# Conv taps handed from GpSimd to VectorE and TensorE, with ScalarE writing the diagonals

## The reference

```python
def conformer_conv(u, dw_w, dw_b, norm_g, norm_b):
    a, gate = jnp.split(u, 2, axis=-1)
    z = a * jax.nn.sigmoid(gate)
    z = depthwise_conv(z, dw_w, width 31, centred) + dw_b     # 512 channels
    return silu(layer_norm(z, norm_g, norm_b))

def attn_conv_mixer(x, ...):
    q, k, v, u = split(x @ w_in)
    q, k = rope(rms_norm(q)), rope(rms_norm(k))               # 8 query heads, 2 key heads
    attn = softmax(q k^T / 8) v
    return concat([attn, conformer_conv(u, ...)]) @ w_out
```

## Time and profile before

| | |
|---|---|
| median of 3 runs (1437.0 to 1439.38) | 1437.44 us |
| the profiled execution: its time | 1439.26 us |
| its span, first to last instruction | 1437.5 us |
| PE busy over the span | 1387.0 us (96%) |
| DVE busy | 663.8 us (46%) |
| ACT busy | 455.4 us (32%) |
| POOL busy | 213.2 us (15%) |
| mean granted clock of PE | 0.988 |

### The profile page before, as it was taken

How to read it: one execution, slowest core, us unless ns; L and a number is a source line. 1 busy time by engine, 2 the same in 40 slices (tenths; PEclk the granted TensorE clock), 3 DMA queues, 4 the chain that set the end, 5 groups by cost and what they waited for, 6 DMA issues and landing times.

```text
span 1437.5 us, 16179 instructions
## 1 busy us (share of the span) xinstructions
PE 1387.0 (96%) x6517; PEld 1152.2 (80%) x6517; DVE 663.8 (46%) x798; ACT 455.4 (32%) x551; POOL 213.2 (15%) x179
## 2 busy tenths in 40 slices
PE   7976799999999999999999999999999999999997
PEld 7864577988888888888888888888888888888886
DVE  4789674743333331175555453654373333332225
ACT  3546562332322311143232332333233222222111
POOL 4467750300000000042202001000030000000000
PEclk9989799999999999999999999999999999999999
DMA  6200002233223323214221212222222333233221
GB/s 212 89 30 30 30 1 69 78 92 113 88 88 116 117 88 108 98 32 151 68 88 58 88 63 83 88 88 89 88 88 88 91 110 91 88 104 130 88 88 59
DMA packets 84014, 124.13 MB, mean 86 GB/s; under 512 B 2689, under 2 KB 61313, under 8 KB 83969
## 3 DMA queue, kind: packets, MB, share of 16 engines
q1 hardware_dynamic: 83968, 123.49, 26.2%
HBM read 121.39 MB, written 2.10 MB: 86 GB/s over the span
## 4 chain that ended last, share of the span: by engine, by line
PE 86%; POOL 6%; DVE 3%; issue 2%; ACT 2%; DMA 0%; POOLq 0%; DVEq 0%; SPq 0%; ACTq 0%
PE ps L1274 22%; PE ps L1275 22%; PE ps L1276 22%; PE ps L1349 19%; POOL acc L499 2%; POOL w_lo L375 2%; PE ps L1287 1%; DVE acc L920 1%; PE ps L1617 0%; ACT tap_part L650 0%; POOL row_inv L557 0%; POOL q_scale L512 0%; ACT w_hi L371 0%; DMA x_tok<-in_x 0%; POOL diag L526 0%
## 5 line engine op out<-in xcount | busy, mean ns | idle before, releaser
L375 DVE TENSOR_TENSOR w_lo<-raw,w_hi 128x2048 fp32r<-128x2048 f32 x101 | 232.6, 2303 | 479.4 <-ACT w_hi L371 479.4
L1274 PE MATMUL ps<-xT_hi,w_hi 128*128 128x512 f32 (+1 forms) x992 | 368.3, 371 | 0.5 <-POOL w_lo L375 0.5
L1275 PE MATMUL ps<-xT_lo,w_hi 128*128 128x512 f32 (+1 forms) x992 | 366.9, 370 | 0.0
L1276 PE MATMUL ps<-xT_hi,w_lo 128*128 128x512 f32 (+1 forms) x992 | 366.6, 370 | 0.0
L371 ACT ACTIVATE w_hi<-raw 128x2048 fp32r<-128x2048 f32 x109 | 208.4, 1912 | 411.9 <-PE ps L1276 236.4
L1274 PEld LDWEIGHTS ps<-xT_hi,w_hi 128*128 128x128 f32 x992 | 187.9, 189 | 32.5 <-POOL w_lo L375 1.1
L1276 PEld LDWEIGHTS ps<-xT_hi,w_lo 128*128 128x128 f32 x992 | 187.8, 189 | 31.8
L1275 PEld LDWEIGHTS ps<-xT_lo,w_hi 128*128 128x128 f32 x992 | 187.8, 189 | 31.1
L575 POOL TENSOR_SCALAR var_eps<-var_eps 128x1 f32<-128x1 f32 x16 | 5.6, 353 | 849.8 <-ACT squares L777 849.8
L1274 PE MATMUL ps<-w_hi,xT_hi 128*128 128x512 f32 (+1 forms) x320 | 121.3, 379 | 0.0
L1276 PE MATMUL ps<-w_hi,xT_lo 128*128 128x512 f32 (+1 forms) x320 | 121.1, 379 | 0.0
(11 more groups left out here) (166 smaller groups left out, 1691.2 us busy)
## 6 DMA issues: line engine op xcount, KB each, us to landing
raw<-in_l_w_in SPq DMA_DIRECT2D x31, 1024.0 KB, 5.2
raw<-in_l_ffn_w_gate SPq DMA_DIRECT2D x22, 1024.0 KB, 5.3
raw<-in_l_ffn_w_up SPq DMA_DIRECT2D x22, 1024.0 KB, 5.3
raw<-in_l_ffn_w_down SPq DMA_DIRECT2D x22, 1024.0 KB, 4.9
raw<-in_l_w_out SPq DMA_DIRECT2D x12, 1024.0 KB, 4.9
x_tok<-in_x SPq DMA_DIRECT2D x4, 512.0 KB, 7.1
out<-x_tok SPq DMA_DIRECT2D x8, 256.0 KB, 2.1
ln_gb<-in_l_ln_mix_g SPq DMA_DIRECT2D x2, 512.0 KB, 5.3
```

The lines of the kernel that those rows point to most:

```text
L375: eng.tensor_tensor(w_lo[ch.s][:], raw[ch.s][:], f32(w_hi[ch.s][:]), ALU.subtract)\
L1274: nc.tensor.matmul(dst, a[0], b[0], start=start, stop=False)
L1275: nc.tensor.matmul(dst, a[0], b[1], start=False, stop=False)
L1276: return nc.tensor.matmul(dst, a[1], b[0], start=False, stop=stop)
```

## The change

GpSimd loses all conv work and the two `w_lo`, and keeps the powers and the pairs' inverses, one after another. VectorE does 73 taps (tiles 0 and 1 and 11 of tile 2), PE 51 (20 of tile 2, 31 of tile 3), at one to two a step by `TAPS_AT`. ScalarE no longer multiplies taps; it writes each diagonal, high and low half, as the identity times the tap's high or low half (`tap_hi`, `tap_lo`), into a ring of eight. VectorE makes the two `w_lo` of the output chunks (steps 10 and 20), does eleven taps ahead of the first query's rope, and takes the rope of query tile 0 ahead of chunk `C_GLU[1]`'s low half. PE turns a pair's inverse two steps later.

```diff
 PAIRS = HEADS // 2
-BATCH = 4
-BATCHES = 8
...
-OUT0_SPLIT_STEPS = (8, 16)
-SIDE_SUM_STEP = 31
+OUT0_SPLIT_STEPS = (10, 20)
+PE_TAPS = 20
+RING = 8
+TAPS_AT = {step: 1 + (step % 2 == 0) for step in range(2, 35) if step != 15}
+CONV_COPY_STEPS = (15, 35)
+TAPS_AT[17] = TAPS_AT[19] = 2
+ON_PE = [(2, k) for k in range(PE_TAPS)] + [(3, k) for k in range(TAPS)]
+assert sum(TAPS_AT.values()) == len(ON_PE)
...
-            added = [0]
-            def add_taps(count):
-                for a in range(added[0], min(added[0] + count, ADDED)):
-                    own_tile = a < TAPS - 1
-                    total = acc[:, 1, :] if own_tile else side_sum[:]
-                    pool.wait_ge(part_tapped, a + (2 if own_tile else 3))
-                    if a:
-                        pool.wait_ge(part_added, a)
-                    nc.gpsimd.tensor_tensor(total, total, tap_part[:, a % 4, :], ALU.add).then_inc(part_added, 1)
-                    added[0] += 1
...
-            add_taps(7)
-            query_scale(0)
-            for t in range(1, TT):
-                add_taps(1)
+            for t in range(TT):
                 query_scale(t)
...
-            for b in range(2):
-                diagonals(b)
-            add_taps(8)
-            def attention_step(s):
-                b = s // 4
-                add_taps(1)
...
-                if s % 4 == 0 and b < BATCHES:
-                    n = min(BATCH, TAPS - BATCH * b)
-                    pool.wait_ge(diag_hi_made, b + 1)
-                    nc.gpsimd.tensor_tensor(diag_lo[:, b % 2, 0:n, :], diag[:, b % 2, 0:n, :],
-                                            f32(diag_hi[:, b % 2, 0:n, :]), ALU.subtract).then_inc(diag_lo_made, 1)
-                    if b + 2 < BATCHES:
-                        diagonals(b + 2)
-                if s >= 9 and s % 8 == 1:
-                    pair_inverse(s // 8 - 1)
-                if s in OUT0_SPLIT_STEPS:
-                    make_lo(pool, Chunk(C_OUT0 + OUT0_SPLIT_STEPS.index(s)), seam_lo_made)
...
-            for s in range(LAST_STEP):
-                attention_step(s)
+            for p in range(PAIRS):
+                pair_inverse(p)
...
-            tapped = [0]
-            def tap_products(count):
-                for n in range(tapped[0], min(tapped[0] + count, TAPS + HANDED)):
-                    ct, k = (1, n) if n < TAPS else (2, n - HANDED)
-                    tap, z = conv_par[:, ct, k:k + 1], zpad[:, ct, k:k + SEQ]
+            diagonals = [0]
+            def tap_diagonals(count):
+                for n in range(diagonals[0], min(diagonals[0] + count, len(ON_PE))):
+                    ct, k = ON_PE[n]
                     if n == 0:
-                        act.wait_ge(par_landed, 16 * 6)
-                        act.wait_ge(z_made, 2)
-                        nc.scalar.activation(acc[:, 1, :], z, ACT.Identity, scale=tap,
-                                             bias=conv_par[:, 1, TAPS:TAPS + 1]).then_inc(part_tapped, 1)
-                    elif n == TAPS:
-                        nc.scalar.activation(side_sum[:], z, ACT.Copy, scale=tap).then_inc(part_tapped, 1)
-                    else:
-                        a = n - 1 if n < TAPS else n - 2
-                        if a >= 4:
-                            act.wait_ge(part_added, a - 3)
-                        nc.scalar.activation(tap_part[:, a % 4, :], z, ACT.Copy, scale=tap).then_inc(part_tapped, 1)
-                    tapped[0] += 1
+                        act.wait_ge(consts_made, 1)
+                        act.wait_ge(tap_lo_made, 1)
+                    if n >= RING:
+                        act.wait_ge(diag_used, n - RING + 1)
+                    nc.scalar.activation(diag_hi[:, n % RING, :], ident[:], ACT.Copy, scale=f32(tap_hi[:, ct - 2, k:k + 1]))
+                    nc.scalar.activation(diag_lo[:, n % RING, :], ident[:], ACT.Copy, scale=tap_lo[:, ct - 2, k:k + 1])\
+                        .then_inc(diag_made, 1)
+                    diagonals[0] += 1
...
-            tap_products(9)
+            act.wait_ge(par_landed, 16 * 6)
+            nc.scalar.activation(tap_hi[:], conv_par[:, 2:4, 0:TAPS], ACT.Copy).then_inc(tap_hi_made, 1)
+            tap_diagonals(RING)
             make_hi(act, Chunk(C_GLU[1]))
             for t in range(TT):
                 query_square(t)
-                tap_products(1 + (t % 2))
             make_hi(act, Chunk(C_GLU[1] + 1))
-            tap_products(2)
             glu_sigmoid(2)
             query_hi(0)
             query_hi(1)
-            tap_products(2)
             glu_sigmoid(3)
             query_hi(2)
             query_hi(3)
             act.preload_act_table(ACT.Exp)
-            tap_products(2)
+            def z_tile_hi(ct):
+                act.wait_ge(z_made, ct + 1)
+                nc.scalar.activation(z_hi[ct][:], zpad[:, ct, :], ACT.Copy).then_inc(z_hi_made, 1)
+            z_tile_hi(2)
...
+                    if s == 2:
+                        act.wait_ge(z_made, CT)
...
-                if s == 0:
-                    z_tile_hi()
-                tap_products(1)
+                if s == 4:
+                    z_tile_hi(3)
+                tap_diagonals(TAPS_AT.get(s - 1, 0))
...
-                b = s // 4
-                if s % 4 == 0 and b < BATCHES:
-                    n = min(BATCH, TAPS - BATCH * b)
-                    act.wait_ge(diag_made, b + 1)
-                    if b >= 2:
-                        act.wait_ge(diag_used, b - 1)
-                    nc.scalar.activation(diag_hi[:, b % 2, 0:n, :], diag[:, b % 2, 0:n, :], ACT.Copy).then_inc(diag_hi_made, 1)
-                if s == TAPS + 3:
-                    act.wait_ge(diag_used, BATCHES)
-                    nc.scalar.activation(acc[:, 3, :], ps[:, CONV_BANK, :], ACT.Identity, bias=conv_par[:, 3, TAPS:TAPS + 1])\
+                if s in CONV_COPY_STEPS:
+                    ct = 2 + CONV_COPY_STEPS.index(s)
+                    act.wait_ge(diag_used, PE_TAPS if ct == 2 else len(ON_PE))
+                    nc.scalar.activation(acc[:, ct, :], ps[:, CONV_BANK, :], ACT.Identity, bias=conv_par[:, ct, TAPS:TAPS + 1])\
                         .then_inc(conv_copied, 1)
                 if s + 1 in OUT0_SPLIT_STEPS:
                     make_hi(act, Chunk(C_OUT0 + OUT0_SPLIT_STEPS.index(s + 1)))
-                if s >= 12 and s % 8 == 4:
+                if s >= 14 and s % 8 == 6:
                     inverse_copy(s // 8 - 1)
-                if s >= 15 and s % 8 == 7 and s // 8 - 1 < PAIRS - 1:
-                    pair_hi(s // 8 - 1)
+                if s >= 16 and s % 8 == 0:
+                    pair_hi(s // 8 - 2)
...
-            taps = [(0, k) for k in range(TAPS)] + [(2, k) for k in range(TAPS - HANDED)]
+            taps = [(ct, k) for ct in (0, 1) for k in range(TAPS)] + [(2, k) for k in range(PE_TAPS, TAPS)]
+            assert len(taps) == DVE_TAPS
...
+                        if (ct, k) == (2, PE_TAPS):
+                            dve.wait_ge(conv_copied, 1)
...
-            conv(2)
+            conv(1)
...
-            conv(6)
-            make_lo(dve, Chunk(C_GLU[1]))
+            dve.wait_ge(tap_hi_made, 1)
+            nc.vector.tensor_tensor(tap_lo[:], conv_par[:, 2:4, 0:TAPS], f32(tap_hi[:]), ALU.subtract).then_inc(tap_lo_made, 1)
+            conv(11)
...
             for t in range(TT):
                 query_rope(t)
-                if t:
+                if t == 0:
+                    make_lo(dve, Chunk(C_GLU[1]))
+                else:
                     query_scaled(t - 1)
                 if t == 2:
...
-            query_lo(0)
-            query_lo(1)
-            conv(3)
-            query_lo(2)
-            query_lo(3)
-            conv(3)
+            for n in range(TT):
+                query_lo(n)
+            conv(4)
...
             row_shift(1)
+            z_tile_lo(2)
...
-                conv(1)
-                if s >= 14 and s % 8 == 6 and s // 8 - 1 < PAIRS - 1:
+                conv(1 + (s % 8 in (0, 1, 3, 4, 6)))
+                if s in OUT0_SPLIT_STEPS:
+                    make_lo(dve, Chunk(C_OUT0 + OUT0_SPLIT_STEPS.index(s)), seam_lo_made)
+                if s >= 15 and s % 8 == 7:
                     pair_scaled(s // 8 - 1)
-                if s >= 16 and s % 8 == 0 and s // 8 - 2 < PAIRS - 1:
+                if s >= 17 and s % 8 == 1:
                     pair_lo(s // 8 - 2)
...
-                k = s - 3
-                if 0 <= k < TAPS:
-                    b, i = k // BATCH, k % BATCH
-                    if k == 0:
-                        pe.wait_ge(z_lo_made, 1)
-                    if i == 0:
-                        pe.wait_ge(diag_lo_made, b + 1)
-                    last = product(ps[:, CONV_BANK, :], (diag_hi[:, b % 2, i, :], diag_lo[:, b % 2, i, :]),
-                                   (z_hi[:, k:k + SEQ], z_lo[:, k:k + SEQ]), k == 0, k == TAPS - 1)
-                    if i == BATCH - 1 or k == TAPS - 1:
-                        last.then_inc(diag_used, 1)
```

(18 more changed lines are left out.)

51 lines of the change are left out of this document (17 added, 34 removed).

## The result

| | before | after |
|---|---|---|
| median | 1438.44 us (1437.0 to 1439.91, 6 runs) | **1416.71 us** (1416.1 to 1417.29, 6 runs) |
| span of the profiled execution | 1437.5 us | 1415.5 us |
| mean granted clock of PE | 0.988 | 0.998 |
| PE busy | 1387.0 us (96%) | 1389.9 us (98%) |
| GpSimd busy | 213.2 us (15%) | 117.6 us (8%) |

The change makes the kernel faster: the ratio is 0.9849 (95% interval 0.9836 to 0.9862), 21.7 us. I had forecast 1416.3.

A forecast was written before the change was run, and what follows sets the result against it. PE was taken as the bound, losing time to waits, stretched VectorE work and low clock. Gains of 8.9 and 12.3 us make 21.2: 1439.26 - 21.2 = 1418.1 for the profiled execution, 1416.3 for the median; range 1410 to 1427.

The forecast's parts named there:

- first stretch: Up to the first scores of step 2, 109.21 us before: they would begin at 100.3, a gain of 8.9 us.
- attention: From scores of step 2 to the conv transposes: 108.0 us before, 95.7 forecast, a gain of 12.3 us.
- a scaling 2.1 to 2.2: VectorE's scaling of a query tile in the first stretch, priced at 2.1 to 2.2 us each, four of them.
- Query transposes and clock: PE's wait of 3.43 us up to 79.00, ahead of the query transposes, would be shortened by 1.7 us.
- A tap 0.66, or 0.78 behind one it depends on: Price in us of one conv tap on VectorE with GpSimd idle; eleven taps ahead of the rope make 8.5.
- Diagonals 0.30 from start to start, 0.40 long: ScalarE's 128-wide products in attention: 0.30 us a piece, about 0.40 us duration each.
- rival B: ScalarE becomes the bound in attention if a small product costs 0.61 us like a wide one: 1428 us; chance 7%.
- Inverses wait for nothing: In attention PE no longer waits for the pairs' inverses; the wait of 14.3 us is gone.
- handing over: Attention's allowance for handing over, 0.05 us a step by choice, 1.6 us in all.
- Rival A: PE's clock falls again in attention: two falls of 6 us, half of it lost, cost 6: 1422 us; chance 15%.
- Rival D: PE and VectorE near their limit don't fit together: a third of a microsecond on 26 steps, 9 us: 1425; chance 11%.
- Rival C: VectorE's taps stay slow because GpSimd isn't what stretches them; at 1.3 us a tap, 1448 us; chance 5%.

The follow-up runs named there:

- loaded kernel: The changed kernel with 24 useless two-array additions on GpSimd that nobody waits for; measured 1426.62 us, ratio 0.9919 to the kernel before.

## Why the prediction was right, step by step

- **Total.** 21.2 us were predicted, 22.0 are measured between the two profiled spans, 21.7 by the medians. That the difference is so small is luck, for two errors of opposite sign stand behind it: the first stretch gained 2.5 us more than forecast (11.4 against 8.9), attention 1.8 less (10.5 against 12.3).
- **First stretch: 8.9 predicted; 12.1 measured from the product of tile 1, 11.4 from the start of the span.** Eleven taps are 8.62 us (8.5) and hidden, the rope waits 1.26 (1.2), a rope is 2.9. The term that was mis-sized is "a scaling 2.1 to 2.2": it is 1.22 to 1.23, four times 0.9 = 3.6 us. I had read it from the row at 76.78, which itself was stretched by one of GpSimd's additions, of the same kind as those whose removal I priced for the taps. The loaded kernel has 1762 ns for it, before 2093. Against the 3.6 stand a rope that began 0.8 late (62.89, forecast 62.1) and 14.1 us in place of 13.8 behind the last scaling, which leaves 2.5.
- **Query transposes and clock.** PE's wait of 3.43 us would be shortened by 1.7, I wrote; it is gone, for the same reason, and with it the fall of the clock at 79.00.
- **A tap 0.66, or 0.78 behind one it depends on.** Held: 756 ns of mean duration. GpSimd as what stretches it is shown by the loaded kernel.
- **Diagonals 0.30 from start to start, 0.40 long.** Held: 0.392. ScalarE is busy 73.1 of 97 us in attention, so rival B doesn't occur. What decided it was the price of a 128-wide product, which I had taken from the growth between 384 and 512 columns.
- **Inverses wait for nothing.** Held.
- **Attention 95.7 us: 97.6 measured.** Of waits I had 4.1 at the start (3.6: 1.39, 0.57, 0.17, 1.48), 1.8 at step 16 (1.76), 0.9 at step 12 (1.81) and 1.6 of handing over. The mis-sized wait is that at step 12. VectorE's timeline has the reason (123.97, in the result section): the low half waits 0.45 us for ScalarE's high half, which I hadn't counted. That is half of what was missing there; the other half isn't traced. Without the waits PE needs 97.6 - 7.4 = 90.2, against my 87.3 and 1.6 of handing over = 88.9. The distances of starts explain the missing 1.3: a listed wait is counted from the end of a row, and so leaves out time. From 125.40 to 127.61 are 2.21 us, 1.98 more than the 0.23 that matmul costs without a wait, and the list has 1.81. Such remainders, and some waits too short to be listed, are 2.5 us in the stretch, so that PE's work alone is 87.7. My 87.3 for it held; waits and handing over are 9.9 where I had 8.4.
- **The range's lower end** names "4.4 us of late waits"; the terms of the sum are 4.1 and 0.9, 5.0 in all, which gives the same 1411.
- **Start: -0.7 us, not in the sum.** Over the fourteen profiles of this study VectorE's product of tile 1 begins between 46.8 and 48.7 us, while from there to the scores of step 2 the nine kernels that have the changed order and a GpSimd without load agree within 0.04 (49.02 to 49.06). So it is scatter between executions, in a stretch whose PE program the change leaves alone.
- **Rival A** (the clock falls again, 15%) was argued away with "the idle times that preceded a fall were 3.43 us and more". That holds for the rows of before and is wrong as a limit: falls came behind 1.39 and 0.57, and behind 1.76, and in the changed kernel's own profile the same waits caused none. Its price was right in direction, too high in size: 1.5 us in one case, 0.24 in the other, not 6.
- **Rival D** (two engines near their limit don't fit together) was half true: each bounds the other in turn. But with 21 of VectorE's taps left out attention is 4.8 us shorter, and my sum already had 5.0 of waits for a late VectorE (4.1 and 0.9); another 9 didn't come.
- **Rival C** never came into question: the tap is fast.

## What to carry to other kernels

An engine that nobody waits for can still be the expensive one: 24 additions on GpSimd, waited for by no one, cost 10 us, mostly by stretching what VectorE does from SBUF; take its work away before you split it more finely. When you remove a disturber, the rows of whatever it stretches are too long as recorded, so take prices for the new kernel from rows where the disturber was idle, for all operations and not just the one that moves. And where two engines are within a few per cent of each other, look for waits with one cause each and move just that piece, to a step where its engine has room; a piece moved within a stretch in which its engine is behind only moves the wait.

## What was not expected of the hardware

- A GpSimd instruction of 128x512 that reads one array stretches VectorE's work by 0.16 us on average, one that reads two by 0.45, although the first takes longer on GpSimd (1811 against 1294 ns).
- Whether the granted clock falls behind the same waits differs between executions: 1.00 throughout in the changed kernel, 0.70 from 104 to 108 us in the kernel with the output weight's halves two steps later, whose PE program is the same up to there. The kernel with the low half ahead of the rope ran on the same chip as the latter, and its clock passed the same 1.39 and 0.57 without falling. What decides it isn't shown.
- A single stretch of low clock can be nearly free, where the engine would have waited for a slower one behind it: 0.24 us in the kernel with the output weight two steps later, for an estimated 1.7 us of lost work (0.87 from 100 to 104 us, 0.70 from 104 to 108).
